# Split-precision products that read the moving tile and write the result from the last column to the first

## What is computed

```python
def first_block(x, c, ctx, ...):
    hx = modulate(rmsnorm(x, g_norm1[l]), mx[0], mx[1])
    hc = modulate(rmsnorm(ctx, g_norm1[l]), mc[0], mc[1])
    px = jnp.split(hx @ w_in[l], IN_SPLIT_IDX, axis=-1)
    pc = jnp.split(hc @ w_in[l], IN_SPLIT_IDX, axis=-1)
    ...
    x = x + mx[2] * (jnp.concatenate([att_x, hg_x], axis=-1) @ w_out[l])
    x = x + mx[5] * swiglu(modulate(rmsnorm(x, g_norm2[l]), mx[3], mx[4]), w_gu[l], w_down[l])
    return rmsnorm(x, g_final)

def second_block(x, positions, ...):
    proj = _rms_norm(x, g_pre_mix[l]) @ w_in[l]
    ...
    merged = gates[..., :D_MODEL] * (a @ w_branch_a[l]) + gates[..., D_MODEL:] * (b @ w_branch_b[l])
    x = x + _rms_norm(merged @ w_out[l], g_post_mix[l])
    m = jnp.square(jax.nn.relu(_rms_norm(x, g_pre_mlp[l]) @ w_up[l])) @ w_down[l]
    return x + _rms_norm(m, g_post_mlp[l])
```

## Time and profile before

| | us |
|---|---|
| median of 3 runs | 822.3 (821.34 to 822.56) |
| the profiled execution | 821.46 |
| its span, first to last instruction | 819.7 |
| matmul engine busy, of the span | 794.3 |
| weight loads busy, of the span | 698.6 |
| VectorE / ScalarE / GpSimd busy, of the span | 427.9 / 418.6 / 377.4 |

### The profile page before, as it was taken

How to read it: one execution, slowest core, us unless ns; L and a number is a source line. 1 busy time by engine, 2 the same in 40 slices (tenths; PEclk the granted TensorE clock), 3 DMA queues, 4 the chain that set the end, 5 groups by cost and what they waited for, 6 DMA issues and landing times.

```text
span 819.7 us, 14292 instructions
## 1 busy us (share of the span) xinstructions
PE 794.3 (97%) x5493; PEld 698.6 (85%) x5493; DVE 427.9 (52%) x684; ACT 418.6 (51%) x641; POOL 377.4 (46%) x181
## 2 busy tenths in 40 slices
PE   5999999999899999999999999999999999999996
PEld 3688877887778999999998889999897999999995
DVE  4575568984667533422336747545356343423435
ACT  5335426455846444444444955654756544444443
POOL 3126000000164654666545996564454554666452
PEclk9999999999999999999999999999999999999998
DMA  9884567133953666555654786444455566566641
GB/s 319 291 287 133 175 229 259 54 103 104 337 177 114 197 194 193 176 179 189 194 165 130 227 211 180 130 107 130 146 166 173 155 181 199 183 187 191 186 152 51
DMA packets 94396, 146.61 MB, mean 179 GB/s; under 512 B 15741, under 2 KB 64110, under 8 KB 94352
## 3 DMA queue, kind: packets, MB, share of 16 engines
q1 hardware_dynamic: 92896, 143.23, 56.0%
q0 software_dynamic: 1424, 2.77, 1.1%
q10 hardware_dynamic: 32, 0.01, 0.0%
HBM read 144.93 MB, written 1.06 MB: 178 GB/s over the span
## 4 chain that ended last, share of the span: by engine, by line
PE 82%; DVE 8%; issue 3%; DMA 3%; POOL 2%; ACT 2%; SPq 0%; DVEq 0%; ACTq 0%; POOLq 0%
PE bank L1878 79%; POOL w_lo L629 2%; PE bank L2148 1%; ACT w_hi L694 1%; DVE hg_at L1433 1%; DVE w_lo L1197 1%; DVE hg_queries L1384 1%; DMA raw<-in_w_in 1%; DMA raw<-in_w_mod 1%; DMA x<-in_x 1%; DMA gate_mlp_b<-gate_rows 1%; PE bank L2456 1%; DVE x L1830 1%; DVE stat L1514 1%; PE bank L1969 0%
## 5 line engine op out<-in xcount | busy, mean ns | idle before, releaser
L629 POOL TENSOR_TENSOR w_lo<-raw,w_hi 128x1024 fp32r<-128x1024 f32 (+2 forms) x150 | 362.2, 2433 | 317.0 <-ACT w_hi L694 316.6
L694 ACT ACTIVATE w_hi<-raw 128x1024 fp32r<-128x1024 f32 (+1 forms) x218 | 226.3, 1046 | 214.2 <-PE bank L1878 188.1
L1197 DVE TENSOR_TENSOR w_lo<-raw,w_hi 128x1024 fp32r<-128x1024 f32 x71 | 87.8, 1247 | 138.0 <-ACT w_hi L694 137.9
L1878 PE MATMUL bank<-z_hi,w_hi 128*128 128x256 f32 x384 | 110.1, 287 | 0.1
L1878 PE MATMUL bank<-z_hi,w_lo 128*128 128x256 f32 x384 | 108.6, 283 | 0.0
L1878 PE MATMUL bank<-z_lo,w_hi 128*128 128x256 f32 x384 | 108.6, 283 | 0.0
L1878 PE MATMUL bank<-n_hi,w_hi 128*128 128x256 f32 x352 | 99.9, 284 | 1.0 <-POOL w_lo L629 1.0
L1878 PE MATMUL bank<-n_hi,w_lo 128*128 128x256 f32 x352 | 99.6, 283 | 0.0
L1878 PE MATMUL bank<-n_lo,w_hi 128*128 128x256 f32 x352 | 99.6, 283 | 0.0
L1878 PE MATMUL bank<-w_hi,mlp_h_hi 128*128 128x512 f32 x216 | 84.4, 391 | 0.0
L1878 PE MATMUL bank<-w_lo,mlp_h_hi 128*128 128x512 f32 x216 | 84.3, 390 | 0.0
(11 more groups left out here) (419 smaller groups left out, 1592.5 us busy)
## 6 DMA issues: line engine op xcount, KB each, us to landing
raw<-in_w_in SPq DMA_DIRECT2D x54, 512.0 KB, 4.7
raw<-in_w_down SPq DMA_DIRECT2D x54, 512.0 KB, 3.8
raw<-in_w_gu SPq DMA_DIRECT2D x44, 512.0 KB, 3.5
raw<-in_w_up SPq DMA_DIRECT2D x32, 512.0 KB, 3.7
raw<-in_w_mod SPq DMA_DIRECT2D x24, 512.0 KB, 4.1
raw<-in_w_mod SPq DMA_DIRECT2D x32, 256.0 KB, 5.8
raw<-in_w_out SPq DMA_DIRECT2D x12, 512.0 KB, 4.3
raw<-in_w_in SPq DMA_DIRECT2D x8, 336.0 KB, 3.1
```

What stands on the lines that cost most here:

```text
L629: nc.gpsimd.tensor_tensor(wl[:, w % SPL, 0:size], raw[:, slot_raw, 0:size], wh[:, w % SPL, 0:size].bitcast(F32), ALU.subtract).then_inc(s_ ...
L694: nc.scalar.activation(wh[:, w % SPL, 0:size], raw[:, slot_raw, 0:size], ACT.Copy).then_inc(s_hi, 1)
L1197: V.tensor_tensor(wl[:, w % SPL, :], raw[:, slot_raw, :], wh[:, w % SPL, :].bitcast(F32), ALU.subtract).then_inc(s_lod, 1)
L1878: return nc.tensor.matmul(out_, l, r_, start=start, stop=stop, skip_group_check=True)
```

## The change

`mm3` turns the views of the result and of both parts of the moving operand round before it issues its three products. The stationary operand is left as it is. Column i of the result still takes column i of the moving operand: both are visited in descending order, so that the same numbers land in the same places. The order of the three products, their waits, their signals and all other instructions are those of before.

```diff
             def mm3(out_, lh, ll, rh, rl, start, stop):
 
+                out_, rh, rl = out_[:, ::-1], rh[:, ::-1], rl[:, ::-1]
                 mm(out_, lh, rh, start, False)
                 mm(out_, lh, rl, False, False)
                 return mm(out_, ll, rh, False, stop)
```

## The result

The changed kernel takes 823.94 us in the median of nine runs (823.15 to 825.59), the kernel before 821.34 us in nine runs beside it (820.30 to 822.56). The ratio is 1.003, with an interval of 1.002 to 1.004: slower by 0.3%. The forecast was no change at 822.3 us. The time lies inside the range that was given, but the nine runs of one kernel do not overlap with the nine of the other, so the case that came true is "slower", which had 0.24. (Of two of the kernels further down, three executions took 1114 to 1573 us against 814 to 826 us for the rest; the times given leave them out.)

The account below looks back on a forecast made before the run. The matmul engine's split products were taken to bound the kernel: 821.46 us profiled plus 0 for the read and 0 for the write, given as the median 822.3 us; own range 820 to 825 us, 8-in-10 range 819.5 to 870.

Parts of the forecast that it names:

- slower: Whole kernel: a measured time above no change by more than about 0.2%, 1.6 us; chance 0.24 over four rivals.
- What bounds the kernel: Matmul engine, busy 97%: the 4194 split products of `mm3` take 647.8 us, 79% of the span, uncovered by other engines.
- The write at no cost: Results of `mm3` written backwards into PSUM: 0 us, because neighbouring columns stay neighbours.
- the two-cycle rival: PSUM end of every split product: a backward write takes two cycles a column, 552 us more, 1374 us; chance 0.05.
- The read at no cost: Moving tile of `mm3` read backwards from SBUF: 0 us, as it leaves a neighbourhood as rarely as forwards.
- One column a cycle and a fixed 13 ns: Price of a split product, from distances of 0.120 us at 256 and 0.226 us at 512 columns.
- A small price: Backward read of split products: 0.13 ns per step across a group of four, 45.5 us more, 867 us; chance 0.10.
- Faster: Split products: the fixed 13 ns shrinks, 8 ns at 256 and perhaps 11 at 512 columns, 785 us; chance 0.04.
- The two larger prices of the read and the write: Split products: write at two cycles, 1374 us, 0.05; fresh read fetch per pair, 1097 us, 0.05, or column, 2020 us, 0.04.
- Turned back: Patterns reversed on both sides are turned back in translation for the chip; forecast's time, chance within no change's 0.72.
- Nothing else moves: Outside the `mm3` patterns: no instruction, wait, transfer, queue, buffer or GpSimd and VectorE work changes; cost 0.

Follow-up runs that it names:

- the streams: Kernel before plus rows of 24 equal products behind its last one, in a bank nobody reads; 512 columns: 228.4 ns forwards, 233.3 ns read back.
- the starts' kernel: Kernel before plus rows of 24 products, moving tile starting 0 to 3 columns on, both directions; forwards at 512 columns 227.1, 236.8, 233.2, 229.0 ns.

## Why the prediction was wrong, point by point

**What bounds the kernel** was right: the loss stands in the distances of `mm3`, and they add up to the change of the span within about 1 us.

**The write at no cost** was right. The kernel that only writes backwards stands at 1.0001 (0.9992 to 1.0010), and the streams that only write backwards are within 0.4 ns of the forward ones at every width. The rule for which the two-cycle rival was kept, in the Trainium skill, Advanced Engine Details and Errata, section PSUM Cachelines, that a pattern which is not contiguous slows matmuls, does not reach descending neighbours: 228.8 ns against 228.4 at 512 columns.

**The read at no cost** is the step that failed: "What counts in the rows is how often the read leaves a neighbourhood, and that is as rare backwards as forwards. I therefore take 0 for the read." The read changed the pace by -1.4 ns in the mean at 256 columns and by about +6 ns at 512, and these make the whole result. How often the read leaves a neighbourhood was not what counts: one and the same forward read takes 227 ns or 233 ns, according to where the tile that is loaded beside it starts. The argument had two holes that the rows of before already showed.

The first is that its rows could not show a small price. The level products are 128 columns wide, and a product of 128 columns stands on a floor of 112 ns, which the streams have at 192 columns too. That a jump for every fourth column costs nothing was read from products that would not have shown a price below that floor. The rows with a price, runs of one and of two, are products that got over it.

The second is that the weight load stood in the text as a busy share, 85% of the span, and nowhere in the price of a product. It also reads SBUF, beside the moving tile of the product ahead of it. A row of the kernel before shows the load for the second product of its triple starting together with the first product, at 700.23 us:

```profile
700.23 0.19 PEld L1878 LDWEIGHTS bank<-z_lo,w_hi 128*128 128x128 f32 x1
```

The runs show that the load takes part in the pace: the stationary tile's start alone took a forward product from 227 to 233 ns (5.40 and 5.53 us), or from 119 to 114. The Trainium skill, SBUF — State Buffer, section Who interferes with whom, gives the matmul engine two read ports, one for the moving operand and one for the weight load, and calls them independent. These runs do not agree: whatever the ports, the place that the load reads from changes the pace of the products.

**"One column a cycle and a fixed 13 ns"** was a coincidence of two numbers. 0.226 us at 512 columns was taken as the rate that the reversed patterns must keep, but it is the rate of one meeting only; of the sixteen stationary starts within 256 bytes most lie at 230 to 234 ns. The 13 ns at 256 columns is near the other end, as most starts there are quicker or equal. And the prediction's own row for 384 columns did not fit: 0.177 us is 17 ns above one column a cycle. The tiles of the kernel before share one place modulo 256 bytes, which suits wide products and not narrow ones. A backward read at 512 columns loses that and gets 233 ns at every contiguous start of the stationary tile (and 235 to 240 at other starts of the moving one); at 256 columns it gets 118 to 120, and there the kernel before had 120.

**The rivals.** "A small price" had the right sign at 512 columns, but its size (16 ns), its sign at 256 columns and its mechanism were wrong: groups in descending order cost as much as groups in ascending order with gaps. "Faster", by a shorter fixed time, came true for the narrow products alone, where no rival had looked for a sign that depends on the width. The two larger prices of the read and the write did not come. "Turned back" is excluded, since the two directions differ.

**Nothing else moves** was right: instructions, waits, the level products and the other engines stayed. That the range held the time is no merit of the argument: the spread given to an unchanged kernel reached to 825 us.

What is shown: the loss and the gain are the read's; a forward read's pace depends on where the loaded tile starts against the moving one; and a loss and a gain of the same kind can be made in the kernel with every read forwards, the loss in the size that was expected, the gain in half of it. What is argued only: that the clash is one of the moving read with the load of the *next* product's columns inside SBUF. No run switches the load off, and no row shows which access waits. What is open: why a read that is backward throughout never reaches 227 ns, and what decides between two paces at the same places.

## What to carry to other kernels

Where split or other one-cycle products run back to back, compare the distance between starts with the number of columns at the granted clock, and try the place of the moving and of the stationary tile modulo 256 bytes, in the kernel itself and not only in streams: a few empty columns were worth 0.7% here, which is more than the reversal moved. Price an edit of a read at each width that the kernel uses, with a row that is not under a floor of another kind; two effects of under 1% each and of opposite sign can read as "no change" on the clock. A rate that looks like "one a cycle and a bit" in one kernel may be the luck of its allocation. And read the single distances, not only their mean: a group's mean here can hide two paces.

## What the runs showed of the hardware

A float32r product takes 111.6 ns at 128 and at 192 columns, read forwards or backwards; at 256 contiguous columns the streams' means are 113.5 to 122.3 ns and at 512 columns 226.6 to 240 ns, by the starts, the direction of the read and the pace that a stream falls into, in kernels whose mean granted clock is 0.998 to 1.00. (The 240 ns are a backward read from column 3 of the starts' kernel.) Two paces can exist at the same places: 226.6 and 233.2 ns at 512 columns with the stationary tile 4 columns on, and about 113 and 118 ns at 256 columns in blocks of one execution. At step 2 each product takes as long as one of twice the columns, 226.9 ns for 256. A PSUM result written in descending order costs nothing (228.8 against 228.4 ns). Alternating the direction from product to product is the worst of the orders that stay with neighbours from column 0, 236.6 ns at 512 columns.
